# A reworked opening, side products inside the projections, w_query loaded by head, and a last tile weighed by columns

## What is computed

```
h = rmsnorm(x, norm1_g);  p = h @ w_in            # q, k (4 heads x 256), v, r (4 x 512), alr (rank 16),
                                                  # cb, cc, cx (conv), ga, gb (2048 each)
loga = log_sigmoid(alr @ w_alpha_up + b_alpha) / 16
o, s_new = gla_chunked(q, k, v, loga, s0)         # S_t = diag(a_t) S_{t-1} + k_t^T v_t, o_t = q_t S_t
y_a = silu(r) * rmsnorm(o, gla_norm_g);  y_b = cb * short_conv(cc * cx)
x = x + (sigmoid(ga) * y_a + sigmoid(gb) * y_b) @ w_out
h2 = rmsnorm(x, norm2_g);  q = h2 @ w_query       # 8 heads x 2 halves x 128
# per head: scores against sub_keys, top 16 of each half, top 16 of the 256 sums -> 16 experts and a softmax g
a = einsum(expert_u[idx], h2);  w = g * gelu(a)
x = x + einsum(w, expert_v[idx]);  y = rmsnorm(x, norm_f_g)
```

## Time and profile before

| | |
|---|---|
| median of 3 runs | 2395.32 us (2395.12 to 2395.39) |
| the profiled execution's own time | 2394.96 us |
| its span, first to last instruction | 2392.9 us |
| mean granted TensorE clock | 0.877 of full speed |
| PE busy | 1798.2 us, 75% |
| PEld busy | 1275.9 us, 53% |
| DVE busy | 1601.2 us, 67% |
| ACT busy | 598.1 us, 25% |
| POOL busy | 930.4 us, 39% |
| moved by DMA | 777.24 MB, mean 325 GB/s |

### The profile page before, as it was taken

How to read it: one execution, slowest core, us unless ns; L and a number is a source line. 1 busy time by engine, 2 the same in 40 slices (tenths; PEclk the granted TensorE clock), 3 DMA queues, 4 the chain that set the end, 5 groups by cost and what they waited for, 6 DMA issues and landing times.

```text
span 2392.9 us, 23881 instructions
## 1 busy us (share of the span) xinstructions
PE 1798.2 (75%) x9151; PEld 1275.9 (53%) x9151; DVE 1601.2 (67%) x2021; ACT 598.1 (25%) x869; POOL 930.4 (39%) x729
## 2 busy tenths in 40 slices
PE   7999999999999999986756565655564455755654
PEld 5999889899899899874422222222221121112221
DVE  4544455646555554386778887879887787687765
ACT  4433554645545543301100000100010010010000
POOL 0000111110111100062655666657656666567662
PEclk9999999999999999998887768778767678887677
DMA  6665787878877767599999999999999999999997
GB/s 185 172 173 165 217 245 234 238 221 232 238 229 218 231 197 188 157 394 378 420 421 422 422 422 421 422 422 395 422 422 422 422 421 422 422 406 413 422 422 301
DMA packets 424341, 777.24 MB, mean 325 GB/s; under 512 B 14024, under 2 KB 344288, under 8 KB 355568
## 3 DMA queue, kind: packets, MB, share of 16 engines
q0 software_dynamic: 89168, 597.86, 60.9%
q1 hardware_dynamic: 333792, 175.71, 27.2%
q10 hardware_dynamic: 1272, 2.18, 0.2%
HBM read 754.51 MB, written 21.25 MB: 324 GB/s over the span
## 4 chain that ended last, share of the span: by engine, by line
PE 46%; DMA 30%; DVE 8%; POOL 8%; issue 5%; ACT 3%; another core or an unknown queue 1%; ACTq 0%; DVEq 0%; POOLq 0%; SPq 0%
DMA ring<-in_expert_v,idx_all 29%; PE bank L1476 11%; PE bank L1477 10%; PE bank L1478 10%; PE bank L1656 8%; POOL ring L640 8%; PE bank L1633 2%; DVE x_tok L1310 2%; DVE ring L1292 2%; ACT w_hi L671 1%; DMA ring<-in_expert_v,idx_s 1%; PE bank L1576 1%; PE bank L1557 1%; PE bank L1462 1%
## 5 line engine op out<-in xcount | busy, mean ns | idle before, releaser
L1656 PE MATMUL bank<-ring,diag 128*128 128x512 f32 x1000 | 670.8, 833 | 489.9 <-DMA ring<-in_expert_v,idx_all 427.0
L1292 DVE CUSTOM_DVE_ANT_0 ring<-ring,xn_tok 128x2048 f32<-128x2048 f32 x256 | 583.6, 2290 | 239.7 <-DMA ring<-in_expert_u,idx_all 232.2
L1656 PEld LDWEIGHTS bank<-ring,diag 128*128 128x128 f32 x1000 | 259.2, 272 | 893.9 <-issue 824.3
L1476 PE MATMUL bank<-act_hi,w_hi 128*128 128x264 f32 x2304 | 663.7, 288 | 1.5 <-DVE w_lo L984 1.5
L1477 PE MATMUL bank<-act_lo,w_hi 128*128 128x264 f32 x2304 | 654.3, 284 | 0.0
L1478 PE MATMUL bank<-act_hi,w_lo 128*128 128x264 f32 x2304 | 653.6, 284 | 0.0
L984 DVE TENSOR_TENSOR w_lo<-raw,w_hi 128x2048 fp32r<-128x2048 f32 x144 | 330.2, 2293 | 347.1 <-ACT w_hi L671 346.7
L640 POOL DMA_INDIRECT ring<-in_expert_u,idx_all x256 | 429.7, 1679 | 287.2 <-DVE g_all L1286 106.5
L640 POOL DMA_INDIRECT ring<-in_expert_v,idx_all x256 | 376.4, 1470 | 299.5 <-PE bank L1656 227.8
L1476 PEld LDWEIGHTS bank<-act_hi,w_hi 128*128 128x128 f32 x2304 | 435.1, 189 | 20.7 <-issue 18.3
L1477 PEld LDWEIGHTS bank<-act_lo,w_hi 128*128 128x128 f32 x2304 | 435.7, 189 | 1.0 <-issue 1.0
(11 more groups left out here) (230 smaller groups left out, 1161.8 us busy)
## 6 DMA issues: line engine op xcount, KB each, us to landing
raw<-in_w_in SPq DMA_DIRECT2D x129, 1024.0 KB, 6.6
s_ring<-in_state_gla POOLq DMA_DIRECT2D x64, 256.0 KB, 6.1
out<-s_ring POOLq DMA_DIRECT2D x64, 256.0 KB, 5.9
raw<-in_w_out SPq DMA_DIRECT2D x16, 1024.0 KB, 6.2
raw<-in_w_query SPq DMA_DIRECT2D x9, 1024.0 KB, 28.2
v_row<-v_samples POOLq DMA_DIRECT2D x32, 256.0 KB, 6.2
xslot<-in_w_query SPq DMA_DIRECT2D x7, 1024.0 KB, 10.5
ring<-in_expert_u,idx_all POOLq DMA_INDIRECT x256, 13.9
```

The lines of the kernel that those rows point to most:

```text
L1292: v.tensor_tensor_reduce(ring[k][:], ring[k][:], xn_tok[:, b // PH, :], 1.0, 0.0, ALU.mult, ALU.add, w_all[:, b * TOPK + s:b * TOPK + s + ...
L1476: mm(out, hi_, act_hi[:, k, :], start=(k == 0), stop=False)
L1656: ins = mm(bank[sum_bank(t) + j][:], diag[nth % N_DIAG][:], ring[k][:, j * 512:(j + 1) * 512], start=first, stop=final)
```

## The change

**Opening.** SyncE's first instructions are the loads of x, tile 1 in two halves; the semaphores are counted later, behind the first weight load. The samples' x is loaded by ScalarE's queue as a full tile of 128 x 128 (`xs_flat`), and so are the parameters, now six transfers. `wau` goes into four strips of 32 rows; `krow` and `crow` follow the first weights. ScalarE squares tile 0 and the samples, VectorE tile 1 in two halves; the table of the root is loaded ahead. The scaling of x is cut into pieces of 512 columns, of which VectorE takes the first two and GpSimd the last two. TensorE starts with 16, 16 and 4 products of the identity with itself (`warm`). The decay ranks no longer go through `w_hi` and `w_lo`: `rank_rows` multiplies unsplit 32-column strips, four of them to the four 32-row strips of one bank, in plain fp32. The first query block (`first_queries`) is split and projected in two halves.

**Projections.** VectorE's split of block 6 moves ahead of the scan of the decays and that of block 7 into it. `project` takes a range of the 16 column blocks: in the heads, the side products of step b stand in the middle of projection b + 1, and the last turn to tokens stands in the middle of the first head's first projection. The state steps are one step earlier (S_BLOCKS), but for the first four of head 0; the products on them stay at the same place, four steps' number (OS_BLOCK) and half a projection. VectorE takes the gate product of the prompt's columns at step 19.

**w_query.** One load is a head, 256 columns, 2 MB; heads 0, 1, 2, 4 and 3 in that order, then 5, 6, 7. Head 4 lies where `w_hi` and `w_lo` were, in the place of two ring buffers, so the ring has six buffers for its first 18 gathers (FEW), and the last two are used from block B_QRY + 10 on. VectorE's `row_tile(0)` moves behind the choice of the first experts.

**Tail.** In the last block TensorE weighs row sets 0, 3, 6, 9, 12, 14 (before 0, 3, 6, 9, 12), VectorE the others, and of the last set VectorE takes columns 0 to 1535 and TensorE the rest (`weigh_rest`). Squares, scaling and the store of tile 1 are cut by columns.

The diff, cut to its core:

```diff
...
-    N_CONSTS, N_LATE_CONSTS = 22, 12
-    N_LINKS = 17
+    N_PAR = 6
+    WARM = (16, 16, 4)
+    STRIP = 32
...
-        xslot = [sb_at(f"xslot{s}", [P, KT, P], F32, at_qk + s * size([P, D])) for s in range(3)]
+        two = 2 * size([P, D])
+        wq_at = (at_qk, at_raw + two, at_raw, at_qk + size([P, D]), at_w, at_raw + two, at_raw, at_qk + size([P, D]))
+        wq = [sb_at(f"wq{h}", [P, KT, 2 * P], F32, at) for h, at in enumerate(wq_at)]
...
+            return s % 2 == 0 if g < N_BLK - 1 else s in (0, 3, 6, 9, 12, 14)
+        LAST, CUT = (N_BLK - 1, TOPK - 1), 1536
...
+        FEW = 6
+        slot_of = [n % FEW if n < 3 * FEW else (n - 3 * FEW) % RING for n in range(len(order_of))]
+        before = [max((z for z in range(max(n - 2 * RING, 0), n) if slot_of[z] == slot_of[n]), default=None)
+                  for n in range(len(order_of))]
+        nth_in_slot = [slot_of[:n].count(slot_of[n]) for n in range(len(order_of))]
...
-        S_BLOCK = [1 + 5 * (m // 4) + m % 4 for m in range(M)]
-        OS_BLOCK = [5 * b + 5 for b in range(M // 4)]
+        S_BLOCKS = [[5 * (m // 4) + m % 4 + (m < 4 and i == 0) for m in range(M)] for i in range(2)]
+        OS_BLOCK = [5 * b + 4 for b in range(M // 4)]
...
+            sp.dma_start(x_tok[:, 0, :], x_p[:, 0, :]).then_inc(x_in[0], 16)
+            for half in range(2):
+                part = slice(half * (D // 2), (half + 1) * (D // 2))
+                sp.dma_start(x_tok[:, 1, part], x_p[:, 1, part]).then_inc(x_in[1 + half], 16)
...
             load(0, win[:, :, COL_ALR:COL_ALR + P])
-            for n in (1, 2, 3):
+            for counter in from_one:
+                sp.sem_inc(counter, ONE)
+            load(1, win[:, :, 0:P])
+            sp.wait_ge(wau_clear, 1)
+            for x in range(4):
+                sp.dma_start(wau[STRIP * x:STRIP * x + RANK, :], w_alpha_up.rearrange("o r n -> (o r) n")).then_inc(wau_in, 16)
...
-                elif Q_SLOTS[j][0] == "r":
-                    sp.wait_ge(lo_done, last_raw(s) + 1)
-                sp.dma_start(q_buf(j)[:], wqry[:, :, j * P:(j + 1) * P]).then_inc(q_landed(j)[0], 16)
+            sp.wait_ge(mm_done, B_OUT + 1)
+
+            def load_query(h):
+
+                sp.dma_start(wq[h][:], wqry[:, :, 2 * h * P:2 * (h + 1) * P]).then_inc(wq_in[h], 16)
+
+            load_query(0)
+            sp.wait_ge(lo_done, B_QRY - 1)
+            load_query(1)
+            sp.wait_ge(lo_done, B_QRY)
+            load_query(2)
+            sp.wait_ge(mm_done, B_QRY)
+            load_query(4)
+            sp.wait_ge(mm_done, B_QRY + 2)
+            load_query(3)
+            for h in (5, 6, 7):
+                sp.wait_ge(mm_done, B_QRY + 2 * (h - 4) + 2)
+                load_query(h)
...
+            pool.wait_ge(rs_done, 1)
+            for part in (2, 3):
+                cols_ = slice(part * 512, (part + 1) * 512)
+                for t in range(2):
+                    g.tensor_scalar(x_tok[:, t, cols_], x_tok[:, t, cols_], rstd[:, t:t + 1], None,
+                                    ALU.mult).then_inc(xp_done, 1)
...
+                if before[n] is None:
+                    if slot_of[n] >= FEW:
+                        pool.wait_ge(mm_done, B_QRY + 10)
+                else:
...
+            act.wait_ge(chain, 3)
+            a.activation(root[:], mean_sq[:], ACT.Sqrt).then_inc(rt_done, 1)
+            act.wait_ge(xs_in, 16)
+            a.activation(xs_junk[:], xs_flat[:], ACT.Square, accum_out=xs_part[:, 0:1]).then_inc(xs_ss, 1)
+            act.wait_ge(x_in[0], 16)
+            a.activation(sq_junk[0][:], x_tok[:, 0, :], ACT.Square, accum_out=ssq[:, 0:1]).then_inc(ss_done, 1)
+            act.wait_ge(ms_done, 1)
...
+            for k in range(KT):
+                act.wait_ge(tr_done, k + 1)
+                a.activation(act_hi[:, k, 0:TP], bank[2 + k % 6][:, 0:TP], ACT.Copy,
+                             scale=pcol[:, 80 + k:81 + k]).then_inc(ah_done, 1)
+                if k == 5:
+                    act.wait_ge(xs_up, 1)
+                    a.activation(act_hi[:, :, TP:T], xs_g[:].rearrange("p (c s) -> p c s", s=TS), ACT.Copy).then_inc(xs_hi, 1)
+            act.sem_inc(hi_done, 1)
+            act.wait_ge(raw_in[1], 16)
+            a.activation(w_hi[1][:, 0:KT // 2, :], raw[1][:, 0:KT // 2, :], ACT.Copy).then_inc(hi_half, 1)
+            a.activation(w_hi[1][:, KT // 2:KT, :], raw[1][:, KT // 2:KT, :], ACT.Copy).then_inc(hi_done, 1)
...
-                    hi(n0 + 2)
+                    if n0 < B_OUT - 1:
+                        hi(n0 + 2)
...
+                act.wait_ge(y_sum, 8 + j + 1)
+                a.activation(xn_tok[:, 1, part], y_tok[:, 1, part], ACT.Square,
+                             accum_out=part_ss[:, j:j + 1]).then_inc(y_ss, 1)
+            act.wait_ge(y_mean, 3)
+            a.activation(root[:, 1:2], mean_sq[:, 1:2], ACT.Sqrt).then_inc(y_root, 1)
...
+                for part in range(2):
+                    cols_ = slice(part * 512, (part + 1) * 512)
+                    for t in range(2):
+                        v.tensor_scalar(x_tok[:, t, cols_], x_tok[:, t, cols_], rstd[:, t:t + 1], None,
+                                        ALU.mult).then_inc(xn_done, 1)
+                    if part == 0:
+                        v.tensor_scalar(xs_n[:], xs_flat[:], rstd[:, 2:3], None, ALU.mult).then_inc(xs_scaled, 1)
...
+                dve.wait_ge(hi_half, 1)
+                v.tensor_tensor(w_lo[1][:, 0:KT // 2, :], raw[1][:, 0:KT // 2, :], w_hi[1][:, 0:KT // 2, :].bitcast(F32),
+                                ALU.subtract).then_inc(lo_half, 1)
+                dve.wait_ge(hi_done, 2)
+                v.tensor_tensor(w_lo[1][:, KT // 2:KT, :], raw[1][:, KT // 2:KT, :], w_hi[1][:, KT // 2:KT, :].bitcast(F32),
+                                ALU.subtract).then_inc(lo_done, 1)
...
+            lo(B_Q + 5)
                 if m == H * KD // 2:
-                    lo(B_Q + 5)
+                    lo(B_Q + 6)
...
+                if b == 19:
+                    dve.wait_ge(oT_ready, ONE + i * 3 + 2)
+                    link(v.tensor_tensor(gate[:, :, 0:TP], gate[:, :, 0:TP], oT[:, :, 0:TP], ALU.mult))
...
+                mine = slice(0, D if (b, s) != LAST else CUT)
+                v.scalar_tensor_tensor(out=y_tok[:, t, mine], in0=ring[k][:, mine], scalar=w_all[:, b * TOPK + s:b * TOPK + s + 1],
+                                       in1=y_tok[:, t, mine], op0=ALU.mult, op1=ALU.add).then_inc(dve_used, 1)
...
-            dve.wait_ge(mm_done, B_QRY + 1)
-            row_tile(0)
             keys_of(0)
             pairs_of(0)
             experts_of(0)
+            dve.wait_ge(mm_done, B_QRY + 2)
+            row_tile(0)
...
+            for half in range(2):
+                part = slice(half * (D // 2), (half + 1) * (D // 2))
+                v.scalar_tensor_tensor(out=y_tok[:, 1, part], in0=y_tok[:, 1, part], scalar=rstd[:, 1:2],
+                                       in1=gf_row[:, part], op0=ALU.mult, op1=ALU.mult).then_inc(y_ready, 1)
...
+                for part, act_ in enumerate((act_hi, act_lo)):
+                    for x in range(4):
+                        k = 4 * g + x
+                        ins = mm(bank[ACC][STRIP * x:STRIP * x + STRIP, 0:T], raw[0][:, k, 0:STRIP], act_[:, k, :].bitcast(F32),
+                                 start=(g == 0 and part == 0), stop=(g == KT // 4 - 1 and part == 1))
+                if g == KT // 4 - 1:
+                    ins.then_inc(mm_done, 1)
+
+            def first_queries():
...
+            pe.wait_ge(consts, 2)
+            warm(WARM[0])
+            pe.wait_ge(consts, 5)
+            for k in range(KT):
+                turn(k)
+                if k == 11:
+                    rank_rows(0)
+                if k == 14:
+                    rank_rows(1)
+            rank_rows(2)
+            rank_rows(3)
+            pe.wait_ge(par_ready, 1)
+            first_queries()
...
             pe.wait_ge(la_ev, H * KD)
             project(B_V)
+            for n0 in range(B_V + 1, B_SIX):
+                project(n0)
+                to_tokens(n0 - 1)
...
-                for c, at in ((0, 9), (1, 17), (2, 23)):
+                for c, at in ((0, 9), (1, 17), (2, 22)):
...
+                    n0 = B_SIX + i * SIX_PER_HEAD + b
+                    project(n0, FIRST)
+                    if n0 == B_SIX:
+                        to_tokens(n0 - 1)
+                    elif b:
+                        beside(i, b - 1)
+                    project(n0, REST)
...
+            def weigh_rest(nth):
+
+                k = ring_slot(V_, *LAST)
+                pe.wait_ge(diag_ready, nth + 1)
+                pe.wait_ge(ring_in[k], landed(V_, *LAST))
+                for j in range(CUT // 512, 4):
+                    ins = mm(bank[sum_bank(1) + j][:], diag[nth % N_DIAG][:], ring[k][:, j * 512:(j + 1) * 512],
+                             start=False, stop=True)
                 ins.then_inc(pe_used, 1)
...
```

402 lines of the change are left out of this document (221 added, 181 removed).

## The result

The changed kernel takes **2331.8 us** (2331.4 to 2333.5, 4 runs) against 2395.2 us before: a ratio of 0.974, 95% interval 0.972 to 0.975. I had forecast 2353 us, with a range down to 2343, so the direction was right and 21 us of gain were missing from my sum.

A forecast was written before the change was run, and what follows sets the result against it. TensorE's unbroken products were taken to bind from 52.8 us, transfers only from about 1019 us; 14.5 + 3.2 + 11.3 + 1.6 + 8 + 3.2 = 41.8 us off 2394.96 gave 2353 us, range 2343 to 2365.

The forecast's parts named there:

- the w_query term: Loads of w_query beside the first gathers: fewer there, in rows of 1 KB, win 8 us (3 to 12).
- opening: From the start to the second query block: earlier loads, norm, turning and ranks win 14.5 us (8 to 17).
- query and value blocks: Projections after the opening: an earlier split of block 6 and a covered turn to tokens win 3.2 us.
- side products and the last turn: In the heads: TensorE's waits get covered, 11.3 us (7 to 13.5), plus 1.6 us at the last head's turn.
- tail: After the last gathers: shorter sums, squares by column, table loaded ahead and halved output win 3.2 us (1.5 to 4).
- the disputed part: In w_query's loads: rows of 512 bytes run at 292 GB/s, rows of 1 KB between that and 422.
- My sign for it: Behind the first gather: 400 GB/s or more for 100 us, and no wait of TensorE for w_query.
- rival (d): Beside the gathers: the sixth head's load lands late and TensorE stands; slower than before, 2425 us; chance 0.03.
- (a): Opening gives half, by serial strips or GpSimd's pieces at 3 us: price 5 to 8, 2359 to 2361 us; chance 0.12.
- (b): In the heads: the side products' waits return as waits for w_lo, up to 11.3 us, 2364 us; chance 0.08.
- (c): In w_query's loads: wider rows give nothing, as 512 bytes already run at line rate; 2357 us; chance 0.09.
- the signs that I had set as limits: Wrong if heads' w_lo waits exceed 3 us, eight strips 2 us, or six-slot gathers fall below 390 GB/s.

The follow-up runs named there:

- the kernel before with 96 bytes: The kernel before with 96 unused bytes ahead of its large arrays, which then start at 19712: 2376.9 us, ratio 0.992.
- at 19840: The changed kernel with its large arrays 128 bytes further: 2353.4 us, ratio 0.983.
- at 19744: The changed kernel with 32 unused bytes ahead of its large arrays: 2357.5 us, ratio 0.984.

## Why the prediction was wrong, point by point

**The step that failed** is a term that the sum does not have: the rate of the gathers. I took the 422 GB/s of the earlier trace rows over into the changed kernel (it stands in the w_query term as 83 us for 35.1 MB) and gave the stage of gathers alone, more than half of the span, no term, which puts it at nothing without a reason. The three small arrays that the change adds, and what they move, the prediction does not mention. The rate rose to 427. The runs put 18.1 us (14 to 23) on the place of the arrays from the side of the kernel before (96 bytes) and 21.5 to 25.7 us from the side of the changed one (128 and 32 bytes). Without it the same edits give 2353.4 us (at 19840) or 2357.5 us (at 19744), the first on my 2353 and both in my range. That the range left it out was not bad luck: no bound in it came from the largest stage. That 2353 is met so closely is in part good luck: the opening's sum, for one, is right by errors that cancel.

| step | forecast, us | measured, us | from |
|---|---|---|---|
| opening | 14.5 (8 to 17) | 14.8 | start of block 3 |
| query and value blocks | 3.2 | 3.5 | starts of blocks 17 and 34 |
| side products and the last turn | 11.3 + 1.6 | 14.4 | starts of blocks 34 and 129 |
| w_query by head | 8 (3 to 12) | 8.0, a remainder | the kernel before with 96 bytes, less the tail |
| tail | 3.2 (1.5 to 4) | 3.7 | last landing to the end |
| place of the arrays | none | 18.1 | the kernel before with 96 bytes |
| sum | 41.8 | 62.5 | span |

**Opening: right sum, two wrong parts, and luck that they cancel.** The turning and what follows it were 1.2 to 3 us later than I rebuilt them; block 2 starts 13.4 us earlier and not 14.5. The scale factors came at 11.8 instead of 10.0 us, since x landed later: VectorE waited 5.24 us and began its first half square at 8.47, where I had it done with both halves at 9.3. ScalarE's square of tile 0, from 6.57 on, was not waited for. Yet the first projections ran at the full clock, so the 1.2 to 1.5 us that I had set aside for them were not spent, and block 2 itself won another 1.5: before, it began with 3.1 us at the lower level, after with none. I had named that row and then not counted what it gives back. GpSimd took 1.67 us a piece (6.69 for 4) where I had allowed 1.5, and TensorE has no row that waits for it. Strips run beside each other: four strips of 264 columns, two passes each, in 0.65 us.

**Side products: right sum, wrong owner.** The waits went as forecast and the new one in head 0 came (2.4 for 2.2). But half a projection of cover, which I had named first for all of them, covers the decayed keys alone; the 9.7 us on the states belong to the earlier states. The heads' gain of 14.4 us is 1.7 more than the waits that left (9.7 + 3.8 + 1.6 - 2.4 = 12.7); no row names that rest.

**w_query: no error found, within wide limits.** The remainder of 8.0 meets the sum, and the disputed part, the price of 512-byte rows, came at 3 to 4.5 us (3.5 forecast); but between placements off the multiple of 256 the whole term comes out at 0.5 to 10. My sign for it, 400 GB/s or more in the 100 us behind the first gather, was met by the place of the arrays: the same edits have 392 GB/s with 32 bytes of pad, and the kernel before has 409 with 96. TensorE never waited for it, and rival (d), which decided at a landing of 115 us, saw at most 62.6.

**Tail:** 3.7 us, 0.5 more than forecast.

**Rivals.** (a), the opening at half, and (b), waits for w_lo, did not come: the only row for w_lo is the opening's 1.6 us. (c), no gain from wider rows, is spoken against by the run with two loads a head. Of the signs that I had set as limits, a gather rate under 390 GB/s while the ring has six slots, waits for w_lo over 3 us, and strips over 2 us a set of eight, none was reached.
